# A one-layer hybrid decode step: low weight halves written over the raw weight ring, index keys prepared earlier, eight value pages in flight

## What is computed

```
xn = rmsnorm(x);  z = xn @ w_in                      # 2048 -> q,k,v, iq(16x64), ik(64), iw(16), cz(2048), ga, gb
s  = sum_h iw_h * relu(iq_h . ik)                    # index scores over past and new keys
sel = top_k(s)                                       # 64 keys for prompt rows, 256 for sample rows
A  = sparse_attend(q, k[sel], v[sel]) @ w_attn_br    # past k and v from cache_k, cache_v by page_table
u  = cz[:1024] * sigmoid(cz[1024:]);  C = silu(layernorm(conv31(u))) @ w_conv_br
h  = x + (sigmoid(ga) * A + sigmoid(gb) * C) @ w_out
y  = h + (silu(hn @ w_gate) * (hn @ w_up)) @ w_down  # hn = rmsnorm(h), inner width 5632
```

## Time and profile before

| what | us |
|---|---|
| median of 3 runs (2247.6 to 2255.72) | 2248.1 |
| profiled execution | 2243.48 |
| its span | 2241.9 |
| PE busy in the span | 2094.9 (93%) |
| DVE busy | 1243.2 (55%) |
| ACT busy | 912.0 (41%) |
| POOL busy | 157.6 (7%) |

### The profile page before, as it was taken

The page is one execution under the profiler, slowest core; times in us unless marked ns, Lnnn a source line. Parts: engine busy times, 40 slices in busy tenths (PEclk is TensorE's granted clock), DMA queues, the critical chain, the costliest instruction groups (busy, mean ns, idle before and its releaser), DMA issues.

```text
span 2241.9 us, 40990 instructions
## 1 busy us (share of the span) xinstructions
PE 2094.9 (93%) x14631; PEld 1975.0 (88%) x14631; DVE 1243.2 (55%) x2258; ACT 912.0 (41%) x1656; POOL 157.6 (7%) x302
## 2 busy tenths in 40 slices
PE   5939998979999799998999999999999999999997
PEld 5925898858888677898999999999999999999997
DVE  4313799734555688884564455554445554445553
ACT  5413443333444322333644454443334443334443
POOL 3410000011111221000000000000000000000012
PEclk9969999979999899999999999999999999999999
DMA  9450254617776599653565555555555555555442
GB/s 244 105 113 1 76 131 133 170 53 224 228 226 198 186 301 303 193 150 96 151 170 158 139 142 150 150 150 150 150 150 150 150 148 150 149 150 149 134 146 72
DMA packets 541456, 346.74 MB, mean 155 GB/s; under 512 B 19298, under 2 KB 520330, under 8 KB 540975
## 3 DMA queue, kind: packets, MB, share of 16 engines
q1 hardware_dynamic: 514480, 259.88, 43.1%
q0 software_dynamic: 25792, 84.46, 11.5%
q10 hardware_dynamic: 1088, 1.05, 0.1%
HBM read 335.24 MB, written 10.83 MB: 154 GB/s over the span
## 4 chain that ended last, share of the span: by engine, by line
PE 61%; DMA 3%; issue 1%; DVE 1%; POOLq 0%; ACT 0%; POOL 0%; DVEq 0%; ACTq 0%
PE psG L1364 19%; PE psG L1365 19%; PE psG L1366 19%; DMA vst<-in_cache_v 3%; PE psS L1361 1%; PE psM L1364 1%; PE psM L1365 1%; PE psM L1366 1%; PE psM L1361 1%; POOLq L427 0%; PE psM L1358 0%; PE psG L1358 0%; DVE stat L1187 0%; DVE OL L1246 0%; ACT L L759 0%
## 5 line engine op out<-in xcount | busy, mean ns | idle before, releaser
L916 DVE TENSOR_TENSOR WL<-RAW,WH 128x512 fp32r<-128x512 f32 x1008 | 681.8, 690 | 708.0 <-ACT WH L545 701.5
L545 ACT ACTIVATE WH<-RAW 128x512 fp32r<-128x512 f32 x1008 | 625.3, 629 | 895.5 <-PE psG L1366 844.9
L1364 PE MATMUL psG<-XH,WH 128*128 128x320 f32 (+1 forms) x2688 | 850.2, 316 | 18.0 <-issue 6.5
L1365 PE MATMUL psG<-XL,WH 128*128 128x320 f32 (+1 forms) x2688 | 839.3, 312 | 0.0
L1366 PE MATMUL psG<-XH,WL 128*128 128x320 f32 (+1 forms) x2688 | 837.0, 311 | 0.0
L1364 PEld LDWEIGHTS psG<-XH,WH 128*128 128x128 f32 x2688 | 507.9, 189 | 54.1 <-issue 36.1
L1365 PEld LDWEIGHTS psG<-XL,WH 128*128 128x128 f32 x2688 | 508.1, 189 | 1.0
L1366 PEld LDWEIGHTS psG<-XH,WL 128*128 128x128 f32 x2688 | 508.6, 189 | 0.0
L1364 PE MATMUL psG<-MH,WH 128*128 128x320 f32 x960 | 302.0, 315 | 0.3 <-DVE ML L1333 0.3
L1365 PE MATMUL psG<-ML,WH 128*128 128x320 f32 x960 | 297.2, 310 | 0.0
L1366 PE MATMUL psG<-MH,WL 128*128 128x320 f32 x960 | 297.2, 310 | 0.0
(11 more groups left out here) (343 smaller groups left out, 1773.1 us busy)
## 6 DMA issues: line engine op xcount, KB each, us to landing
RAW<-in_w_in SPq DMA_DIRECT2D x160, 512.0 KB, 5.1
RAW<-in_w_ffn_gate SPq DMA_DIRECT2D x88, 512.0 KB, 4.7
RAW<-in_w_ffn_up SPq DMA_DIRECT2D x88, 512.0 KB, 4.6
RAW<-in_w_ffn_down SPq DMA_DIRECT2D x80, 512.0 KB, 4.3
kst<-in_cache_k POOLq DMA_DIRECT2D x64, 512.0 KB, 4.0
vst<-in_cache_v POOLq DMA_DIRECT2D x64, 512.0 KB, 5.4
RAW<-in_w_out SPq DMA_DIRECT2D x32, 512.0 KB, 5.0
RAW<-in_w_attn_br SPq DMA_DIRECT2D x16, 512.0 KB, 5.0
```

What stands on the lines that cost most here:

```text
L545: act.activation(WH[:, s % 2, 4 * r:4 * r + 4], RAW[:, s, 4 * r:4 * r + 4], ACT.Copy).then_inc(hi_done, 1)
L916: dve.tensor_tensor(WL[:, s % 2, k], RAW[:, s, k], WH[:, s % 2, k].bitcast(F32), ALU.subtract).then_inc(lo_done, 1)
L1364: pe.matmul(out, WH[:, s % 2, k], hi, start=start, stop=False)
L1365: pe.matmul(out, WH[:, s % 2, k], lo, start=False, stop=False)
```

## The change

- **Ring.** `WL` is no tile of its own any more but another name for `RAW`: the low half is written over the raw weight, four slots deep. So a slot may be reloaded only when PE has multiplied its unit, and SP waits for `mm_done` instead of `lo_done`.
- **ikiw.** Its narrow tiles are converted only as wide as they are, and the empty quarters get a small copy of zeros. The last part of the down projection loads 8 + 8 row tiles, overlapping, instead of 8 + 4.
- **Start.** POOL issues the index-key pages as soon as the page table is there, two samples' worth before the write of `xTs` to scratch and six after it. DVE zeroes `iqs` and `IW` once that write has landed; ACT waits for this (`pool_zero`) before its first iq unit.
- **Index keys.** `ikb` and a new `ikTa` for all 8 samples are filled in iq: after each iq unit from the second on PE transposes one sample's 8 pages, the eighth after the first ikiw unit.
- **Index stage.** No POOL staging: PE reads `iqs` and `IW` in place. The new tokens' scores of all samples go first, the samples' scores use two pairs of banks in turn, and the matmuls of zeros are gone. POOL waits for the bias table's write only before it loads `Tb`.
- **Top-k.** Of the 32 sample rounds, qk has 8 (even units), v 8, cz 16.
- **Pages.** Eight value pages in flight.
- **Seams.** The two waits before gbB and out and the zeros in out are gone; the channel sums come after the second gbB unit; `hT` is loaded when the convolution branch's low halves are done (`cl_dn`).

```diff
             def load(G_, s, dst_a, src_a, dst_b, src_b, first=False):
                 if not first:
-                    sp.wait_ge(lo_done, 16 * G_ + (4 * s - 12))
+                    sp.wait_ge(mm_done, 16 * G_ + (4 * s - 12))
...
+    T["WL"] = nc.alloc_sbuf_tensor_at("WL", [P, 4, KT, P], F32R, offset=where["RAW"])
...
-                dve.tensor_tensor(WL[:, s % 2, k], RAW[:, s, k], WH[:, s % 2, k].bitcast(F32), ALU.subtract).then_inc(lo_done, 1)
+                dve.tensor_tensor(WL[:, s, k, c], RAW[:, s, k, c], WH[:, s % 2, k, c].bitcast(F32), ALU.subtract).then_inc(lo_done, 1)
...
             pool.wait_ge(a_bias, 1)
             pool.dma_start(gscr.ap(), gsb[:, None, :].to_broadcast([H, P, RELW])).then_inc(g_wr, 16)
-            pool.wait_ge(g_wr, 16)
-            pool.wait_ge(d_iw, 1)
-            pool.wait_ge(d_cpA, 1)
+            pool.wait_ge(d_ikt, 1)
...
+            pool.wait_ge(g_wr, 16)
             pool.dma_start(Tb[:], bass.AP(tensor=gscr, offset=P - 1, ap=[[RELW - 1, P], [P * RELW, H], [1, NP]])).then_inc(tb_ld, 16)
...
                 for s in range(4):
                     ahead(G0["qk"] + g, s)
-                    take8(m8s[:], Ws[:])
+                    if s % 2 == 0:
+                        take8(m8s[:], Ws[:])
...
-            pool.wait_ge(ml_dn, KT)
+            pool.wait_ge(cl_dn, CT)
             for i, (a, b) in enumerate([(0, 4), (4, KT)]):
                 pool.dma_start(hT[:, a:b, :], xscr.rearrange("(k p) n -> p k n", p=P)[:, a:b, :]).then_inc(h_ld[i], 16)
...
-            for s in range(2):
-                pe.wait_ge(ev[s], 2 * G0["gbB"] + 1)
             for u in range(4 * GN["gbB"]):
                 x_out(G0["gbB"] + u // 4, u % 4)
-                if u == 0:
+                if u == 1:
                     pe.wait_ge(yc_done, 2 * CT)
...
-            for s in range(2):
-                pe.wait_ge(ev[s], 2 * G0["out"] + 1)
             total_sq = MB[0][:, 0:NQ]
-            zero(total_sq, True)
```

More of the change, by code:

```diff
@@ L498, in _ @@
             pool.wait_ge(lg_done, B)
-            pool.sem_inc(v_used, 4)
-            v_pages = pages(vst, cache_v, v_ld, v_used)
+            pool.sem_inc(v_used, 8)
+            v_pages = pages(vst, cache_v, pg_ld, v_used)
             v_pages(0)
@@ L951, in _, with keys @@
             lo(0, 1)
-            def ring(name):
-                def body(g):
-                    for s in range(4):
-                        ahead(G0[name] + g, s)
-                loop(dve, GN[name], body)
-            ring("iq")
+            dve.wait_ge(x_wr, 16)
+            dve.memset(iqs[:], 0.0)
+            dve.memset(IW[:], 0.0).then_inc(pool_zero, 1)
+            def keys(b):
+                dve.wait_ge(ik_tr, b + 1)
+                dve.tensor_copy(ikTa[:, b, 512:PAST], TB[1][:]).then_inc(d_cpD, 1)
+            for u in range(4 * GN["iq"]):
+                if u >= 2:
+                    keys(u - 2)
+                ahead(G0["iq"] + u // 4, u % 4)
             dve.wait_ge(a_tab, 1)
@@ L966, in _ @@
                 dve.tensor_copy(bT7[:, c], SB[1][:, 0:Q * H].rearrange("p (q h) -> p h q", q=Q))
-                ins = dve.tensor_copy(bNw[:, c], TB[0][0:NS, 0:Q * H].rearrange("p (q h) -> p h q", q=Q))
+                ins = dve.tensor_copy(bNw[:, c], SB[1][0:NS, P:P + Q * H].rearrange("p (q h) -> p h q", q=Q))
             ins.then_inc(a_bias, 1)
-            ring("ikiw")
+            for s in range(4):
+                ahead(G0["ikiw"], s)
+                if s % 2 == 0:
+                    keys(6 + s // 2)
             dve.wait_ge(d_setup, 1)
@@ L1474, in _ @@
                 products(G0["ikiw"], s, range(8), 8, product)
+                if s == 0:
+                    keys(B - 1)
             for s in range(2):
@@ L1524, in idx @@
-            def idx(g, last=False):
-                b = g * 2
-                scores(b, 0)
-                keys(b + 1, 1)
-                total(b, 0)
-                scores(b + 1, 1)
-                if not last:
-                    keys(b + 2, 0)
-                total(b + 1, 1)
-            keys(0, 0)
-            loop(pe, B // 2 - 1, idx)
-            idx(B // 2 - 1, True)
-            for out in sums:
-                ins = zero(out, False)
-            ins.then_inc(sum_mm, 1)
+                mm(G[0][0:NS, :], iw_of(b), rl[:, b % 2, 0:512], b == 0, b == B - 1)
@@ new lines, in total @@
+                mm(G[1][0:NS, :], iw_of(b), rl[:, b % 2, 512:PAST], b == 0, b == B - 1).then_inc(sum_mm, 1)
+            for b in range(B):
+                ins = mm(MB[0][:, Q * b:Q * b + Q], iq_of(b), ikT[:, NP + Q * b:NP + Q * b + Q])
+            ins.then_inc(n_mm, 1)
+            scores(0)
+            scores(1)
+            pe.wait_ge(d_rln, 1)
+            for b in range(B):
+                mm(MB[1][0:NS, 0:Q], iw_of(b), rln[:, Q * b:Q * b + Q], b == 0, b == B - 1)
+            for b in range(B):
+                total(b)
+                if b + 2 < B:
+                    scores(b + 2)
@@ L1801, in squares @@
                 pe.wait_ge(h_sq, g * 4 + (s + 1))
-                mm(total_sq, ones[:], sq2[:, s % 2, :], False, False).then_inc(h_st, 1)
+                first, last = isinstance(g, int) and g == 0 and s == 0, isinstance(g, int) and g == GN["out"] - 1 and s == 3
+                mm(total_sq, ones[:], sq2[:, s % 2, :], first, last).then_inc(h_st, 1)
             lagged_all(GN["out"], lambda g, s: split_hidden(G0["out"] + g, s), squares)
-            zero(total_sq, False).then_inc(h_st, 1)
             for n, (k0, m) in enumerate(PARTS):
```

257 lines of the change are left out of this document (120 added, 137 removed).

## The result

| | us |
|---|---|
| before, median (2247.6 to 2255.7) | 2250.5 |
| changed, median of 4 runs (2192.3 to 2193.6) | 2192.9 |
| ratio, 95% interval | 0.974 (0.972 to 0.976) |
| changed, profiled execution | 2192.3 |
| its span | 2190.8 |

The change saves 58 us; 2173 with a range of 2158 to 2191 was forecast. The time lies just over the range and 20 us over the forecast. From profile to profile it saves 51 us where 75 were summed up, so 24 us of the sum are missing. (The median of before lay 7 us over its profiled execution, that of the changed kernel does not.)

What follows compares the result with a forecast made beforehand. PE was taken as full in the feed-forward part, so gains had to come where it waits. Terms of -75.1 us took 2243.5 to 2168.4 for a profiled execution; with 4.6 added, the median forecast was 2173 us, range 2158 to 2191.

Steps and rivals of the forecast that it cites:

- Ring: Weight slots now freed by PE: price 0, hidden by 12 us, as long as L is under 19.7 us.
- L: Weight ring: time from a slot's freeing to the landing of both halves, taken as at most 7.0 us.
- my rival of the starved ring: Feed-forward part: L over 19.7 us makes each of 136 units wait; at L = 23, 2286 us; chance 0.02.
- Index stage: From setup's end to the stage's end: 81.5 us becomes 36.2, 45.3 us less; -37.2 with start and moved transposes.
- The start and the keys in iq: Start, iq and ikiw: key transposes 8.6 us more, start 1 us more, narrow ikiw conversions 1.5 us less.
- qk and v: With top-k rounds moved to cz, PE becomes the bound in qk: qk -9.7 us, v -7.1 us.
- two units in 16.0 us: qk: PE's pace without a gap, 8.0 us a unit, used to put 14 units at 111.7 us.
- cz: cz takes over top-k rounds; DVE has 109 us free, 8 more rounds cost it 21: 0 (to +3).
- ga: Eight value-page slots remove all PE waits for pages, -7.2 us; at worst nothing or a few us of loss.
- The estimate of 27 us for a unit's weights: ga: a unit's 128 weight descriptors per engine would take 27 us if taken descriptor for descriptor with pages.
- Seams, zeros: Waits before gbB and out go, -8.6 and -4.7 us; the zeros at the end go, -0.6 us.

Runs made afterwards that it cites:

- the late write: Changed kernel with one line moved: POOL waits for the prompt's index keys before it issues the bias table's write, not after; 2163.8 us, ratio 0.963.

## Why the prediction was wrong

**Ring.** This step failed. It said "Price 0, and hidden by 12 us", from L, the time from a freed slot to the landing of both halves, of at most 7.0 us in the feed-forward part. Over the 135 units there it held: 925.1 us both times. But I wrote L down as one number for the whole kernel. At the first qk unit L was 33 us, because the write of the table stood before it, and the collision there costs 23.9 us (96.6 against 72.7 without it), as much as the 24 us missing from the sum. The mechanism is that of my rival of the starved ring, at one place instead of 136. I had both halves of it on the page: the write takes 35.9 us, and the changed kernel issues it sooner and the weights later. I costed the moved write for POOL, and not for the queues that its bytes share. Where I looked at two queues at work, in ga, neither was starved; but a page packet takes 0.16 us there (0.578 x 16 x 120 us / 6778), and one of the write's 0.745.

**Index stage.** Apart from that it was right: 73.7 forecast for its stretch, 72.7 measured, and for the scores and sums by themselves 36.2 forecast and 35.9 measured (134.5 to 170.4 us with the late write). The start and the keys in iq came to +8.2 against +8.1, but part of that is luck: iq's end moved by 5.9 us where six groups of keys and the start made 7.4, and ikiw by 2.3 where two groups less 1.5 made 0.6.

**qk and v.** The mechanism was right, the size was not. The "two units in 16.0 us" were the last two of a group of four. PE's own pace is 32.7 us for a group of four (9.3, 7.4, 8.0, 8.0), so 8.2 a unit, and the first of the 14 took 10.0: 116.1. A pace has to be read over a whole turn of the loop. For v it is the same on a smaller scale: 63.8 against 62.9, its first unit taking 9.3.

**cz.** "0 (to +3)" was wrong, at -9.4. I took "PE is 210.2 of 219.4 us busy" for a bound; of the 9 idle us some 6 were waits of up to 0.6 us for `kTs` and 3 without a releaser that the profile shows, and all of them went with the move of the top-k steps ahead of the low halves. That move is in the diff between the kernels; I read it as part of the division of the rounds.

**Attention.** It had no term, since nothing in it changed. It took 8.5 us more, with 17 us more at the half clock.

**ga.** -9.9 against -7.2: the listed waits were all of one kind, but short ones don't show as idle time. The eight slots gave 12.4, and the later loads took some of it back. The estimate of 27 us for a unit's weights did not come about: a half landed in a median of 6.2 us there, with the DMA engines at 0.96 and PE full. It was an estimate from the rule of the Trainium skill (DMA: Bandwidth & Descriptors, section on queues, rings and completion order); its two packet times come from rows 9, not 8, and give 0.16 us for a page, not 0.18. **Seams, zeros:** right to 0.1 us each.

The errors of qk, v and the attention (4.4, 0.9 and 8.5 us too hopeful) and those of cz, ga and some tenths (9.4, 2.7) nearly cancel, so the sum missed by the collision alone, and the range had no room for 24 us. That the others cancel is luck: each of the two stretches priced at nothing was off by more than 8 us.

## What to carry to other kernels

When a change frees a long DMA to start sooner, list what is loaded from its start to its end, with the engines that stand in order behind those loads; a mean DMA share of a half is no proof of room. A prefetch whose release moves has to be checked against each long transfer, not against the usual landing time. And where PE's work is a chain of small steps, look at the clock at its start: six matmuls in an idle time of a few us were worth 13 us of the stretch here, and 8 between the medians, with runs that spread by as much.

## What the runs showed of the chip

Where the table's write and the weights met, they changed places packet by packet, 4.8 KB in 745 ns against 512 bytes in 27 ns, and the weights moved nothing from 126 to 130 us and 0.07 MB in the 16 us from 130 on, although the write kept only about half of the engines busy. Two such writes at once kept nearly all of them busy (97%) and moved 54 GB/s against 49 for one. SP's queue stood as well: an issue that takes 0.4 us in this stretch with the late write took 21.8. And the half clock lasted 13.5 to 34 us in the same code.
